# A fused two-block forward pass: first norm ahead of its modulation, constants in two parts, first GQA scores ahead of the last key block, output in four transfers

## What is computed

```python
# first layer: x (256 x 1024), one conditioning vector c
ada = jax.nn.silu(c) @ w_ada + b_ada
shift1, scale1, gate1, shift2, scale2, gate2 = [a[:, None, :] for a in jnp.split(ada, 6, axis=-1)]
hn = _rmsnorm(h, norm1_g) * (1.0 + scale1) + shift1
# then hn @ w_in for everything: dt and gates, x, z, B, C, q, k, v
...
# GQA: q (16 heads of 64), k, v (4 groups of 64), norms per head, rope; softmax(q k^T) v
...
return rms_norm(x, final_norm_g)      # the output, 256 x 1024
```

## Time and profile before

| | |
|---|---|
| three runs | 2043.56, 2042.8, 2044.27 us; median 2043.56 |
| the profiled execution's own time | 2044.59 us |
| its span, first to last instruction | 2042.8 us |
| PE busy | 1939.3 us, 95% of the span |
| DVE, ACT, POOL busy | 1024.7 us (50%), 560.9 us (27%), 59.3 us (3%) |
| mean granted TensorE clock | 0.985 of full speed |
| DMA | 357.30 MB, 175 GB/s over the span |

### The profile page before, as it was taken

One profiled execution on the slowest core, in us unless ns is written; L12 is line 12 of the kernel. 1 busy time (PEld: TensorE's weight loads), 2 busy tenths in 40 slices (PEclk: granted clock), 3 DMA queues, 4 the chain that ended last, 5 costly groups with the idle time before them and its releaser, 6 DMA issues.

```text
span 2042.8 us, 27370 instructions
## 1 busy us (share of the span) xinstructions
PE 1939.3 (95%) x9945; PEld 1362.7 (67%) x9945; DVE 1024.7 (50%) x2285; ACT 560.9 (27%) x1177; POOL 59.3 (3%) x68
## 2 busy tenths in 40 slices
PE   5999999999989999999999899999999899999997
PEld 4887787758745555554565488888444465788886
DVE  2366573387332222334587877776788325333311
ACT  3433400181221111131273233332000235244310
POOL 0000000000000000000000001100000010000000
PEclk8999999989999999999999999999999999999999
DMA  9444484415559999830203222223765030144441
GB/s 385 151 186 191 180 350 176 167 50 206 212 218 426 425 426 419 329 145 0 83 1 111 96 91 94 82 82 118 278 261 196 11 106 1 42 145 161 168 188 37
DMA packets 39469, 357.30 MB, mean 175 GB/s; under 512 B 4295, under 2 KB 9038, under 8 KB 10318
## 3 DMA queue, kind: packets, MB, share of 16 engines
q1 hardware_dynamic: 39374, 356.04, 44.5%
HBM read 354.97 MB, written 1.05 MB: 174 GB/s over the span
## 4 chain that ended last, share of the span: by engine, by line
PE 90%; DVE 4%; issue 2%; DMA 2%; ACT 1%; PEld 1%; DVEq 0%; SPq 0%; ACTq 0%; PEldq 0%
PE bank L647 49%; PE bank L1396 13%; PE bank L1167 7%; PE bank L1152 4%; PE bank L1189 4%; PE bank L768 2%; PE bank L1361 1%; PE bank L1271 1%; PE bank L1279 1%; DMA ring<-in_ada 1%; PE bank L1128 1%; PE bank L1368 1%; PE bank L873 1%; DVE ring L2085 1%; DMA ring<-in_gs 1%
## 5 line engine op out<-in xcount | busy, mean ns | idle before, releaser
L647 PE MATMUL bank<-hn,ring 128*128 128x256 f32 (+2 forms) x2080 | 516.0, 408 | 9.6 <-ACT hn L1493 8.0
L647 PE MATMUL bank<-arena,ring 128*128 128x256 f32 (+2 forms) x1600 | 467.3, 449 | 17.6 <-issue 13.8
L647 PEld LDWEIGHTS bank<-hn,ring 128*128 128x128 f32 (+1 forms) x2080 | 396.2, 191 | 120.1 <-issue 69.0
L647 PEld LDWEIGHTS bank<-arena,ring 128*128 128x128 f32 (+1 forms) x1600 | 297.7, 188 | 180.5 <-issue 147.9
L1396 PE MATMUL bank<-ring 128*128 128x256 f32 x704 | 159.8, 380 | 2.4 <-DVEq L2768 0.9
L1396 PEld LDWEIGHTS bank<-ring 128*128 128x128 f32 x704 | 132.9, 190 | 22.5 <-issue 2.1
L1972 DVE SCALAR_TENSOR_TENSOR bank<-ring,c_rows 128x1024 f32<-128x1024 f32 x96 | 118.1, 1230 | 23.2 <-DMA ring<-in_ada 17.9
L1396 PE MATMUL bank<-hn,ring 128*128 128x256 f32 x528 | 122.7, 382 | 3.8 <-ACT hn L1833 3.8
L1972 DVE SCALAR_TENSOR_TENSOR ring<-ring,c_rows 128x1024 f32<-128x1024 f32 x96 | 117.1, 1220 | 0.0
L1473 ACT ACTIVATE hn<-resid 128x256 f32<-128x256 f32 (+1 forms) x48 | 22.6, 485 | 336.4 <-DVE resid L2063 336.4
L1396 PEld LDWEIGHTS bank<-hn,ring 128*128 128x128 f32 x528 | 101.3, 192 | 18.6 <-issue 4.6
(11 more groups left out here) (424 smaller groups left out, 2098.4 us busy)
## 6 DMA issues: line engine op xcount, KB each, us to landing
ring<-in_ada SPq DMA_DIRECT2D x28, 2048.0 KB, 8.7
ring<-in_up SPq DMA_DIRECT2D x44, 1024.0 KB, 4.8
ring<-in_egu SPq DMA_DIRECT2D x20, 2048.0 KB, 11.0
ring<-in_edn SPq DMA_DIRECT2D x39, 1024.0 KB, 9.5
ring<-in_down SPq DMA_DIRECT2D x16, 1408.0 KB, 9.6
arena<-in_egu SPq DMA_DIRECT2D x10, 2048.0 KB, 10.6
hn<-in_egu SPq DMA_DIRECT2D x9, 2048.0 KB, 11.0
ring<-in_adat SPq DMA_DIRECT2D x8, 2048.0 KB, 12.5
```

Of the source, the lines that this page charges most:

```text
L647: last = mm(out, lhs(i), rhs(i), start=i == 0, stop=i == k - 1)
```

## The change

**Constants.** Their order is changed so that seven (identity, ones and five of one or two columns) stand first, up to column CW_FIRST = 262. SP loads these first, where it loaded all 2734 columns; the other 2472 are a fourth transfer of `rest_landed`, behind `w_small` and ahead of the first x chunk. **First norm.** DVE waits for `std_ready` and computes the inverse before the first ada copy; behind the ada copies it multiplies the blocks of x with rstd (3, 3 and 2 blocks); after the modulation one tensor_scalar for each block multiplies and adds, and raises `hn_ready`. ACT's `shifted` for this norm is gone. **GQA.** `end_phase` moves ahead of `values_of(1)` and block_step(1, KVG) on PE, ahead of the value copy on ACT, and ahead of block_step(1, KVG) on DVE; these steps run as the extra steps of round 1. **Output.** SP waits for the blocks two by two and issues four transfers; it waits for them, and then for the phase.

```diff
--- before.py
+++ after.py
@@ -65,12 +65,14 @@
 NSLOT = 6
 
 
-CONSTS = [("ident", P), ("ones", P), ("tri", P), ("trix", P), ("mneg", 2 * P), ("below", P), ("halves", P), ("pnsa", P),
-          ("pgqa", P), ("dup0", P), ("dup1", P), ("pmla", QK), ("invf", 1), ("eps", 1), ("eps64", 1),
-          ("gcos", T), ("gsin", T), ("mcos", T), ("msin", T), ("cneg", 2 * NCMP), ("c01", 2 * NCMP),
-          ("rev4", NG), ("rev8", EPG), ("place", 1), ("fold", 2)]
+CONSTS = [("ident", P), ("ones", P), ("invf", 1), ("eps", 1), ("eps64", 1), ("place", 1), ("fold", 2),
+          ("tri", P), ("trix", P), ("mneg", 2 * P), ("below", P), ("halves", P), ("pnsa", P),
+          ("pgqa", P), ("dup0", P), ("dup1", P), ("pmla", QK), ("gcos", T), ("gsin", T), ("mcos", T), ("msin", T),
+          ("cneg", 2 * NCMP), ("c01", 2 * NCMP), ("rev4", NG), ("rev8", EPG)]
 CO, _o = {}, 0
 for _n, _w in CONSTS:
+    if _n == "tri":
+        CW_FIRST = _o
     CO[_n] = (_o, _w)
     _o += _w
 CW = _o
@@ -104,7 +106,8 @@
 PI_BELOW = 3.1415925
 
 NSA_QUERIES, MOE_PHASE, GQA_QUERIES, MLA_LOW_RANK, LAST_PHASE = 4, 8, 9, 11, 14
-SETUP_DMAS, REST_DMAS, LATE_DMAS = 1 + VT + 2, 3, 5
+HN_READY = 72
+SETUP_DMAS, REST_DMAS, LATE_DMAS = 1 + VT + 2, 4, 5
 
 
 class Pair:
@@ -484,7 +487,7 @@
                 for _, sl, _ in plan:
                     used[sl] += trips
 
-            sp.dma_start(consts[:, :], dr["consts"]).then_inc(setup_landed, 16)
+            sp.dma_start(consts[:, 0:CW_FIRST], dr["consts"][:, 0:CW_FIRST]).then_inc(setup_landed, 16)
             for v in range(VT):
                 r = min(P, VR - v * P)
                 sp.dma_start(vec_rows[0:r, v, :], dr["vecs"][v * P:v * P + r, :]).then_inc(setup_landed, 16)
@@ -507,6 +510,7 @@
             sp.dma_start(rows32[:, 0:2 * HEADS], dr["ssm_rows"]).then_inc(rest_landed, 16)
             sp.dma_start(rows32[:, 3 * HEADS:], dr["route_rows"]).then_inc(rest_landed, 16)
             sp.dma_start(w_small, dr["w_small"].rearrange("p (k n) -> p k n", k=KD)).then_inc(rest_landed, 16)
+            sp.dma_start(consts[:, CW_FIRST:], dr["consts"][:, CW_FIRST:]).then_inc(rest_landed, 16)
             stream(1, [("x", 1, at(0)), ("z", 0, at(0)), ("bc", 2, at(0))])
             sp.dma_start(c_row, dr["c_rows"][:, 0:D].rearrange("p (a t) -> p a t", a=4)).then_inc(late_landed, 16)
             sp.dma_start(c_rows[:, :, :], dr["c_rows"][:, D:3 * D].rearrange("p (v d) -> p v d", v=2)).then_inc(late_landed, 16)
@@ -609,9 +613,12 @@
                 else:
                     stream(2, [("down", q, (lambda q: lambda i: i * 4 + q + 8)(q)) for q in range(4)])
 
+            out = dr["out"].rearrange("p (k t) -> p k t", k=KD)
+            for k in range(0, KD, 2):
+                sp.wait_ge(s["hn_ready"], HN_READY - KD + k + 2)
+                sp.dma_start(out[:, k:k + 2, :], resid[:, k:k + 2, 0:T]).then_inc(s["stored"], 16)
+            sp.wait_ge(s["stored"], 16 * (KD // 2))
             sp.wait_ge(phase, 3 * LAST_PHASE)
-            sp.dma_start(dr["out"].rearrange("p (k t) -> p k t", k=KD), resid[:, :, 0:T]).then_inc(s["stored"], 16)
-            sp.wait_ge(s["stored"], 16)
 
 
         @block.tensor
@@ -1253,11 +1260,14 @@
                             block_step(b, g)
                     values_of(0)
                     block_step(0, KVG)
-                    values_of(1).then_inc(s["v_mm"], 1)
-                    free(0)
-                    taken(1, 0)
-                    block_step(1, KVG)
                     end_phase(False)
+
+                    def last_block():
+
+                        values_of(1).then_inc(s["v_mm"], 1)
+                        free(0)
+                        taken(1, 0)
+                        block_step(1, KVG)
 
                     def gqa_pair(g, b, qt):
                         nk = 4 if qt < 2 else 2
@@ -1283,7 +1293,8 @@
 
                         return Pair(scores, values, tiles=[k * P for k in range(nk)])
 
-                    attention([gqa_pair(g, b, t) for g in range(KVG) for b in range(2) for t in (0, 2, 1, 3)], 4, 16, 8)
+                    attention([gqa_pair(g, b, t) for g in range(KVG) for b in range(2) for t in (0, 2, 1, 3)], 4, 16, 8,
+                              ahead=[last_block])
                     end_phase(False)
                     gemm(2, (1, 3), 2, KD, lambda k: o2[:, k, :], T2, attended(8, lambda k: k, lambda k: o2[:, k, :]))
                     taken(2, 0)
@@ -1447,6 +1458,7 @@
                 gemm(2, (0, 1, 2, 3), 1, FB, act_block, w)
             late_norm(T)
             normed()
+            assert n["hn_ready"] == HN_READY
             end_phase()
 
 
@@ -1550,8 +1562,6 @@
             act_e.wait_ge(s["rope_reduced"], 1)
             fn(nsin[:, :], ang, ACT.Sin)
             fn(ncos[:, :], tmp_rope, ACT.Sin).then_inc(s["rope_sin"], 1)
-            act_e.wait_ge(s["ada_ready"], 1)
-            shifted(T, 0, 0)
 
 
             act_e.wait_ge(s["dt_pe"], 1)
@@ -1785,10 +1795,14 @@
                         for b in range(3):
                             block_step(b, g)
                     block_step(0, KVG)
-                    act_e.wait_ge(s["v_mm"], 2)
-                    fn(gva[:, 0:2, :], bank[6][:, :], ACT.Copy).then_inc(s["v_ready"], 1)
                     end_phase(False)
-                    attention([Pair(branches=1, w=512 if t % 2 == 0 else 256) for t in range(32)], 16)
+
+                    def sequence_values():
+
+                        act_e.wait_ge(s["v_mm"], 2)
+                        fn(gva[:, 0:2, :], bank[6][:, :], ACT.Copy).then_inc(s["v_ready"], 1)
+
+                    attention([Pair(branches=1, w=512 if t % 2 == 0 else 256) for t in range(32)], 16, {1: sequence_values})
                     end_phase(False)
                 else:
                     for b in range(2):
@@ -2135,15 +2149,22 @@
                 ve.drain()
             ve.drain().then_inc(s["rope_reduced"], 1)
             ve.wait_ge(s["csil_ready"], 1)
+            ve.wait_ge(s["std_ready"], norms[0] + 1)
+            inverse(rstd[:, 0:T], T, hn[:, KD - 1, :], hn[:, KD - 2, 0:16])
+            norms[0] += 1
             for q in range(4):
                 if q == 3:
                     ve.wait_ge(s["ada_cols"], 1)
                 ada_copy(q, q, q % 3)
+                for k in range(3 * q, min(3 * q + 3, KD)):
+                    V.tensor_tensor(hn[:, k, 0:T], resid[:, k, 0:T], rstd[:, 0:T], ALU.mult)
             ve.wait_ge(s["ada_cols"], 4)
             ada_bias(0, bank[4][:, 0:32], 4, 0, 1, VO["b_ada"])
             ve.drain()
             modulate(0, 0, 1, VO["norm1_g"])
-            norm(T, lambda part: mod[0][:, 0, part, :], hn, True)
+            for k in range(KD):
+                V.tensor_scalar(hn[:, k, 0:T], hn[:, k, 0:T], mod[0][:, 0, 0, k:k + 1], ada[0][:, k, 0:1],
+                                ALU.mult, ALU.add).then_inc(s["hn_ready"], 1)
             n["sq_ready"] += KD
 
 
@@ -2610,11 +2631,10 @@
                     for g in range(KVG):
                         for b in range(3):
                             block_step(b, g)
-                    for b in range(2):
-                        block_step(b, KVG)
+                    block_step(0, KVG)
                     end_phase(False)
                     attention([Pair(branches=1, w=512 if t % 2 == 0 else 256) for t in range(32)], 4, 16,
-                              lambda g, b: V.tensor_copy(o2[:, g, :], b))
+                              lambda g, b: V.tensor_copy(o2[:, g, :], b), {1: lambda: block_step(1, KVG)})
                     end_phase(False)
                     gemm(T2, 16, 1, out_ada)
                 else:
```

## The result

Four runs of each kernel side by side: the changed one took 2033.15 us (median, 2030.89 to 2034.45), the one before 2043.18 (2039.88 to 2044.27). The ratio is 0.9947, 95% interval 0.9936 to 0.9959: faster by 10.8 us of 2043.2 (8.4 to 13.1), where 8.1 had been forecast. (This ratio isn't the quotient of the two medians, whose difference is 10.0 us.) Measured again later beside 11 runs of the kernel before (2043.4), six runs of the same changed kernel gave 2035.02 and a ratio of 0.9955 (0.9943 to 0.9968), 9.2 us. The profiled executions took 2044.59 and 2033.56 us, their spans are 2042.8 and 2031.8.

A forecast was written before the change was run, and what follows sets the result against it. The prediction took PE to bound the kernel (90% of the chain), with gains only where PE waits. Start 4.0, GQA 1.8 and output 2.3 summed to 8.1 us, taking the median from 2043.56 to 2035.4, range 2032.5 to 2039.0.

The forecast's parts named there:

- Part 1: Front of the load queue: splitting the constants lets x and the ada chunks land earlier, 2.2 us.
- Part 2: First norm: inverse and products hidden ahead of the modulation, no ACT shift behind it; dt product starts 2.1 us earlier.
- clock at the start: Early dt product: PE's clock falls again for about as long, the projection starts later relative to its rise; costs 0.3 us.
- Part 3: GQA seam: reordered handovers bring the first values earlier; bounds 1.3 and 2.3 us, 1.8 taken.
- Part 4: Output tail: three quarters are stored before the last of four transfers is issued; 2.3 us.
- clock stretch's 1.0: GQA seam: 1.0 of the scheduled 2.3 us is the clock at 0.50, which a shift may move elsewhere.
- upper bound (3.0): Load queue's front: if limited by bytes all along, 1.27 MB fewer at 420 GB/s gain 3.0 us.
- Rival C: Start: queue front bound by issues, or PE waits for the second constants; 2036.6 to 2037.4 us, chance 0.15.
- rival B: Start: clock stays up through dt product and x projection, about 4 us more, 2031.4 us; chance 0.10.
- bound of 2.6: Output tail: the upper of two bounds on the gain from four transfers, the lower being 1.5 us.
- rival D: Tail: four output transfers run one after the other, each with its fixed part; 2042.8 us, chance 0.07.
- E: Whole kernel: shifted PE waits leave the clock longer at 0.50, making it slower, 2048 us; chance 0.03.

The follow-up runs named there:

- x5_seam: Kernel before, with four unread products on PE while it waits for the first exp at the GQA seam; 2043.11 us, ratio 0.9993.
- experiment 1: Kernel before with one part of the change at a time: constants 2040.17 us, norm 2040.11, GQA 2040.14, output 2041.0.
- x2_half: Changed kernel with half of the constants' second part (618 KB) loaded with the first, ahead of vectors and x; 2032.8 us, ratio 0.9949.
- x4_merged: Changed kernel with DVE's eight products x times rstd written as three instructions; 2032.98 us, ratio 0.9944.
- x3_busy: Changed kernel with three unread products on PE between the column turns and the dt product; 2029.56 us, ratio 0.9935.
- x7_all: Changed kernel with two vector transfers, merged norm products, half the constants' second part loaded first, and two unread PE products before the dt product; 2031.21 us, ratio 0.9937.

## Why the prediction was right or wrong

Direction, places and order of the handovers were right, and both medians of the changed kernel (2033.15 and 2035.02) lie in the range of 2032.5 to 2039.0; the sum of 8.1 us was too small, since the two measurements gave 10.8 and 9.2. By the terms, each with what the runs showed:

| term | forecast | measured |
|---|---|---|
| Part 1, constants | 2.2 | 2.5 (means of 5 and 6 profiles) |
| Part 2, norm | 2.1 | 1.6 |
| clock at the start | -0.3 | 0.3 (means of 5 and 7 profiles), 1.1 in the first profile |
| Part 3, GQA | 1.8 | 2.5 |
| Part 4, output | 2.3 | 2.5 |
| sum | 8.1 | 9.4 |

The first two profiles lie 11.0 us apart, 2.9 more than the sum. Of these, 1.3 are the terms above, 0.7 chance in the landing of x and 0.8 chance in the clock.

**The step that failed most is Part 3's "I take 1.8, the middle".** The step-by-step schedule had given 2.3, with the clock stretch's 1.0 in it, and it was right: counted from the end of values_of(0), the first values came after 13.32 us where the schedule has 13.54, and the events between them stand within 0.4 us of it. The 1.3 that was to remain if the stretch only moved was right as well: x5_seam gives the schedule 1.4. Wrong was to take the middle between them: 1.8 where 2.5 was measured. The same text named what brings the stretch on, PE waits that shrink (2.37 us for the first exp before, 0.44 after), and the four kernels of experiment 1 show it present with the long wait and absent with the short ones; x5_seam, with the long wait filled, has none either. Where two bounds differ by one event, the term is one bound or the other, not half of it. The next largest misses are the clock at the start (-0.3 where 0.3 was measured, with no row behind the -0.3) and Part 2 (2.1 where 1.6 was measured), which went the other way.

**Part 1.** The upper bound (3.0) was nearer than I gave it, but its reason holds only in part: bytes are saved at the queue's rate only until something else binds, and putting 618 KB of the 1236 back cost nothing (x2_half). SP's issues got shorter (3.21 us for the seven vector transfers instead of 3.81, x issued at 4.87 instead of 5.46), which the prediction named as a possibility and didn't price; that is 0.6 of the 2.5 us at most. Rival C as an issue-bound front held partly in mechanism, not in its price. What sets the rest is open. The last ada chunk landed at 7.47 + 22.93 = 30.4 instead of 31.4.

**Part 2.** The count of instructions, their durations (0.33 each; forecast 0.35) and their cover between the ada copies were right. What was missing was a stop that no row of before could show: 0.43 us of issue ahead of the modulation, gone in x4_merged. 2.1 - 0.43 = 1.7, and 1.6 was measured. The constants' landing, forecast 1.1 us ahead of need, came 0.3 ahead, and in x4_merged it bound PE.

**The clock at the start.** It fell again about the start of the dt product, as forecast, and rival B did not occur. By "TensorE: Matmul & The Clock Gate" of the Trainium skill, section "HAM oscillation", idle gaps bring it down, and the prediction took from it that a gap of 1.0 us would not. The gap was 1.54 us, and the clock fell in all seven profiles with the norm part and no added products. x3_busy, with the gap filled, agrees with that rule; x7_all, where PE was idle for 0.14 us and it fell for 10.2 us, shows that more belongs to it here. The 0.3 taken back had no row behind it; over twelve profiles the term is 0.3 in the other direction, and two single profiles give anything from -1.0 to 1.8.

**Part 4.** 2.5 of a bound of 2.6: the last transfer kept 3.1 us behind the last scaling (6.35 - 3.25). The transfers overlapped, so rival D did not come about: four of 256 KB end 2.5 us sooner than one of 1 MB, because the bytes move while DVE works (277 GB/s between 2027.0 and 2028.7, when the last scaling ends). The advice of 1 MiB or more per DMA in "DMA: Bandwidth & Descriptors" of the Trainium skill, section "Rules for kernel authors", would have kept the one transfer; it is given there for bandwidth, and here the end of the last transfer counts. The fixed cost of about 2 us in the Trainium skill's section "Anatomy of one DMA" of the same title is given for transfers issued by GpSimd, while SP issues these; here the fixed parts did not add up. Five end later than four. E, a longer time at 0.50, did not occur: 51.7 us in the profile of the changed kernel, 59.8 in that of before.

**The range.** Its low end lay 2.9 us under the number; it is called halfway to B, but halfway between 2035.4 and 2031.4 is 2033.4, and with that the first median, 2033.15, would lie outside. So it is partly luck that the range held. Repeated, the kernel's ratio moved from 0.9947 to 0.9955, 1.6 us, as much as the error of the forecast's sum (1.3).

## What to carry to other kernels

Judge an edit of 2 us by the distance between two named events in the trace, which repeats to 0.1 us, and not by the median, which for the same kernel moved by 2. Read the first landing and the start-up clock over several profiles before you believe a difference there. Where a clock stretch hangs on a wait that the edit shortens, count it as wholly gone or wholly left: at the seam, with waits of 0.7 us or less left, it went; at the start, with 1.5 us left, it stayed. And look at the waits that stand just behind the one you remove: here the constants landed 0.3 us ahead of the first block and bound PE as soon as the norm was 0.4 us shorter, and behind the clock's stretch stood the landing of the x chunk.

## What the runs showed of the hardware that I had not expected

- DVE stopped 0.5 us ahead of the modulation with nothing awaited, in all seven profiles with the products as eight instructions (0.51 to 0.53), and in none of the three with three.
- Issues on SP took longer behind more bytes, but not in proportion: seven vector transfers 3.73 to 3.90 us behind 1367 KB of constants, 3.21 behind 749 KB (x2_half) and behind 131 KB.
- PE's first instruction scattered from 12.55 to 14.01 us among kernels whose loads up to it were the same, and only from 10.64 to 10.89 once the constants were split.
- Three products of 0.5 us that nobody reads gave 2.6 to 3.7 us at the start (x3_busy); in a kernel whose dt product could start 1.3 us earlier the clock fell inside them for 3.4 us, and with two of them for 10.2.
